# HGRN2 score levels: two chunks per product with one chunk's keys reversed, and keys and prefixes of later groups on ScalarE

## What is computed

```python
def hgrn2_chunk(S, inp):
    q, k, v, logf = inp
    G = jnp.cumsum(logf, axis=2)
    diff = G[:, :, :, None, :] - G[:, :, None, :, :]
    decay = jnp.exp(jnp.where(causal[None, None, :, :, None], diff, -jnp.inf))
    A = jnp.einsum('bhtd,bhtsd,bhsd->bhts', q, decay, k)
    o = jnp.einsum('bhts,bhsv->bhtv', A, v) + jnp.einsum('bhtd,bhdv->bhtv', q * jnp.exp(G), S)
    G_last = G[:, :, -1]
    S_new = jnp.exp(G_last)[..., None] * S + jnp.einsum(
        'bhsd,bhsv->bhdv', k * jnp.exp(G_last[:, :, None, :] - G), v)
    return S_new, o
```

## Time and profile before

| | us |
|---|---|
| runs: median (lowest to highest) | 708.96 (708.69 to 710.48) |
| profiled execution | 710.52 |
| its span, first to last instruction | 708.8 |
| busy in the span: TensorE products | 691.4 |
| TensorE weight loads | 661.7 |
| VectorE | 425.1 |
| GpSimd | 353.6 |
| ScalarE | 304.5 |
| mean granted TensorE clock | 0.995 of full speed |

### The profile page before, as it was taken

One profiled execution on the slowest core, in us unless ns is written; L12 is line 12 of the kernel. 1 busy time (PEld: TensorE's weight loads), 2 busy tenths in 40 slices (PEclk: granted clock), 3 DMA queues, 4 the chain that ended last, 5 costly groups with the idle time before them and its releaser, 6 DMA issues.

```text
span 708.8 us, 13435 instructions
## 1 busy us (share of the span) xinstructions
PE 691.4 (98%) x4822; PEld 661.7 (93%) x4822; DVE 425.1 (60%) x998; ACT 304.5 (43%) x860; POOL 353.6 (50%) x461
## 2 busy tenths in 40 slices
PE   7999999999999999999999999999999989999995
PEld 6799999999999999999999999999999988888884
DVE  5835346279882362698923645989336158776257
ACT  6644541635543516345444254455452343232333
POOL 5753233357572343476724333768243368765423
...
## 3 DMA queue, kind: packets, MB, share of 16 engines
...
## 4 chain that ended last, share of the span: by engine, by line
PE 84%; DVE 5%; POOL 3%; issue 2%; DMA 2%; SPq 1%; ACT 1%; POOLq 0%; DVEq 0%; ACTq 0%
PE proj L277 45%; PE proj L296 10%; PE mix L1720 5%; PE mix L1751 3%; PE mix L2197 3%; PE mix L2169 2%; PE mix L2209 2%; PE mix L2171 2%; PE mix L1701 2%; PE mix L896 1%; PE mix L1695 1%; PE mix L887 1%; PE mix L902 1%; PE mix L822 1%; PE mix L1691 1%
## 5 line engine op out<-in xcount | busy, mean ns | idle before, releaser
L277 PE MATMUL proj<-uTh,w_high 128*128 128x352 f32 (+4 forms) x768 | 261.7, 341 | 0.0
L277 PE MATMUL proj<-uTh,w_low 128*128 128x352 f32 (+4 forms) x768 | 245.7, 320 | 0.0
L277 PE MATMUL proj<-uTl,w_high 128*128 128x352 f32 (+4 forms) x768 | 245.3, 319 | 0.0
L277 PEld LDWEIGHTS proj<-uTh,w_high 128*128 128x128 f32 x768 | 145.1, 189 | 0.2
L277 PEld LDWEIGHTS proj<-uTl,w_high 128*128 128x128 f32 x768 | 145.1, 189 | 0.0
L277 PEld LDWEIGHTS proj<-uTh,w_low 128*128 128x128 f32 x768 | 144.3, 188 | 0.0
L322 POOL TENSOR_TENSOR w_low<-w_raw,w_high 128x256 fp32r<-128x256 f32 (+1 forms) x54 | 73.1, 1355 | 52.5 <-DVE decay L370 26.8
L1292 POOL TENSOR_TENSOR f_suffix<-f_suffix,f_prefix 128x192 f32<-128x192 f32 x84 | 54.3, 647 | 26.5 <-DVE f_prefix L1512 19.5
L1720 PEld LDWEIGHTS mix<-level_x 128*127 128x127 f32 (+6 forms) x448 | 54.3, 175 | 5.3 <-issue 2.9
L1720 PE MATMUL mix<-level_x 128*127 128x64 f32 (+6 forms) x448 | 54.1, 253 | 0.8 <-DVE level_x L1503 0.8
L1560 DVE SCALAR_TENSOR_TENSOR conv_out<-conv_in,hg_taps,conv_out 128x352 f32<-128x352 f32 (+2 forms) x81 | 52.5, 648 | 0.5
...
## 6 DMA issues: line engine op xcount, KB each, us to landing
...
```

The lines of the kernel that those rows point to most:

```text
L277: last = pe.matmul(acc[:, 0:tw], w[j % 2][:, k, :], u[:, k, t0:t0 + tw], start=(k == 0 and i == 0), stop=(k == KT - 1 and i == 2))
```

## The change

It does five things.

1. **Level products.** `X` becomes two pairs of tiles. `XK` (256 columns) holds chunk 0's keys in its first 128 columns; in its second 128 columns the even-block keys of chunk 1 stand in their places and those of chunk 2 in reversed order, which puts them on the places of the odd blocks. `XQ` (192 columns) holds the odd queries densely. One product of `XK`'s second half with the 128 queries of chunks 1 and 2 gives both chunks' scores; chunk 0 has a product of its own from group 1 on. The keys are no longer cut. GpSimd writes the even keys in two instructions, the second in reverse.
2. **Reversed tokens of chunk 2.** So that the scores of each group's last chunk have reversed keys throughout, `back` (128 columns) holds that chunk's reversed keys for m = 0 and then its reversed values for the transpose; `kf` is written in two instructions, its last 128 columns in reverse.
3. **Masks.** `mask_st` becomes `mask_diag`, `mask_odd` (with a reversed one for the last chunk, made by `flipped_masks` on GpSimd between two weight splits of the front phase) and `mask_lv` for the GDN phases; VectorE makes 15 copies in place of one cast.
4. **ScalarE makes keys and prefixes of groups 1 and 2** (`affine`), and the reversed blocks (`keys_back`, and a copy of the reversed values once the gram step 0 is done). VectorE's `start` remains for group 0.
5. **The squares** write to `on` instead of to a tile of their own.

```diff
-        pool.tensor_copy(mask_st[:, 0, :], ident[:, :]).then_inc(consts, 1)
+        for c in range(GC - 1):
+            pool.tensor_copy(mask_diag[:, c, :], ident[:, :]).then_inc(consts, 1)
...
+        def flipped_masks():
+
+            pool.memset(flipped[:, 0:LEVELS, :], 1.0).then_inc(flip_step, 1)
+            pool.memset(flip_diag, 0.0).then_inc(flip_step, 1)
...
+            for i in range(LEVELS):
+                b = 1 << i
+                pool.affine_select(out=cells(i), in_=cells(i), compare_op=ALU.is_ge, fill=0.0, base=b - P,
+                                   pattern=[[2 * b, P // (2 * b)], [0, b]], channel_multiplier=1).then_inc(flip_step, 1)
...
         early_low(3)
+        flipped_masks()
         early_low(4)
...
-        dve.tensor_copy(mask_st[:, 1:LEVELS + 1, :], mwork[:, 0:LEVELS, :])
+        for i in range(LEVELS):
...
+            for c in range(GC - 1):
+                dve.tensor_copy(mask_odd[:, i, c, :].rearrange("p (n b) -> p n b", b=b), odd)
+        dve.tensor_copy(mask_lv[:, :, :], mwork[:, BASE:LEVELS - 1, :])
...
-        X = [sb(f"level_x{i}", [P, GW], F32, st) for i in range(2)]
+        XK = [sb(f"level_k{i}", [P, 2 * P], F32, st) for i in range(2)]
+        XQ = [sb(f"level_q{i}", [P, GW // 2], F32, st) for i in range(2)]
+        back = sb("hg_back", [P, P], F32, st)
...
+            for t in XK:
+                pool.memset(t[:, 0:P], 0.0)
...
-                    xv_, kv_, sv_ = (halves(t[:, first(g):GW], b) for t in (X[n % 2], kk, suf))
-                    if i == 0:
-                        pool.tensor_copy(xv_[:, :, 0, :], kv_[:, :, 0, :]).then_inc(x_even, 1)
-                    else:
+                    if i:
                         pool.wait_ge(suf_done, n)
-                        pool.tensor_tensor(xv_[:, :, 0, :], kv_[:, :, 0, :], sv_[:, :, 0, :], ALU.mult
-                                           ).then_inc(x_even, 1)
+                    flipped_k = XK[n % 2][:, P:2 * P][:, ::-1]
+                    for dst, cs in ((XK[n % 2][:, first(g):2 * P], slice(first(g), 2 * P)), (flipped_k, slice(2 * P, GW))):
+                        xv_, kv_, sv_ = (halves(t, b)[:, :, 0, :] for t in (dst, kk[:, cs], suf[:, cs]))
+                        if i == 0:
+                            last = pool.tensor_copy(xv_, kv_)
+                        else:
+                            last = pool.tensor_tensor(xv_, kv_, sv_, ALU.mult)
+                    last.then_inc(x_even, 1)
...
-                pool.tensor_tensor(kf[:, :], kk[:, :], suf[:, :], ALU.mult).then_inc(kf_done, 1)
+                pool.tensor_tensor(kf[:, 0:2 * P], kk[:, 0:2 * P], suf[:, 0:2 * P], ALU.mult)
+                pool.tensor_tensor(kf[:, 2 * P:GW][:, ::-1], kk[:, 2 * P:GW], suf[:, 2 * P:GW], ALU.mult).then_inc(kf_done, 1)
...
+            def affine(dst, src, a, b):
+                return act.activation(dst, src, ACT.Identity, scale=fc[:, a:a + 1], bias=fc[:, b:b + 1])
+
+            def keys_back(g):
+                affine(back[:, :], hth[:, (g + 1) * GW - P:(g + 1) * GW][:, ::-1], 2, 1).then_inc(k_back, 1)
+
+            act.wait_ge(par, 3)
+            keys_back(0)
...
+                    if m == 0:
+                        full(act, plan, ("gram", g, 0))
+                        act.copy(back[:, :], hv[:, (g + 1) * GW - P:(g + 1) * GW][:, ::-1]).then_inc(v_back, 1)
...
+                if g + 1 < NG:
+                    act.wait_ge(qf_done, g + 1)
+                    act.wait_ge(tot_set, g + 1)
+                    affine(pre[:, :], hth[:, (g + 1) * GW:(g + 2) * GW], 1, 0).then_inc(pre_set, 1)
                 act.copy(vtok[:, :], full(act, plan, ("tv", g))[:, 0:GW]).then_inc(bank_free(plan, ("tv", g)), 1)
+                if g + 1 < NG:
+                    keys_back(g + 1)
+                    act.wait_ge(kf_done, g + 1)
+                    affine(kk[:, :], hth[:, (g + 1) * GW:(g + 2) * GW], 2, 1).then_inc(fk, 1)
                 act.copy(ktok[:, :], full(act, plan, ("tk", g))[:, 0:GW]).then_inc(bank_free(plan, ("tk", g)), 1)
...
-                if g + 1 < NG:
-                    start(g + 1)
...
-                        else:
-                            both = X[(LEVELS * g + m - 1) % 2][:, chunk(i)]
-                            keys = max(P - (1 << (m - 1)), HALF)
-                            last = pe.matmul(ap[0:keys, i * P // 2:(i + 1) * P // 2], both[:, 0:keys],
-                                             halves(both, 1 << (m - 1))[:, :, 1, :], start=True, stop=True)
+                    else:
+                        n = LEVELS * g + m - 1
+                        keys, odd = XK[n % 2], XQ[n % 2]
+                        if g:
+                            pe.matmul(ap[:, 0:P // 2], keys[:, 0:P], odd[:, 0:P // 2], start=True, stop=True)
+                        last = pe.matmul(ap[:, P // 2:GW // 2], keys[:, P:2 * P], odd[:, P // 2:GW // 2], start=True, stop=True)
```

82 lines of the change are left out of this document (51 added, 31 removed).

## The result

Twenty runs of each kernel: before 708.97 us (708.48 to 711.01), after **710.47 us** (709.65 to 711.58), ratio 1.0017 with a 95% interval of 1.0011 to 1.0023. That is slower by 1.2 us (0.8 to 1.6), inside the 0.3% that I called no change. I had forecast 704.1, with a range of 700.4 to 709.4: the sign and the range were both wrong. The profiled execution took 711.58 us, its span is 709.9 (before: 708.8).

A forecast was written before the change was run, and what follows sets the result against it. TensorE, busy 98% of the span, was taken as the bound. Terms -7.8 - 1.2 + 0.8 + 3.0 + 0.3 = -4.9 us, from a median of 708.96, gave 704.1 us, range 700.4 to 709.4.

The forecast's parts named there:

- The products: Joined level products on TensorE: -7.8 us over eight groups (1 and 2, four heads), -1.2 in the last head's group 0.
- In groups 1 and 2 [...] it is the bound: TensorE, busy 23.10 of 23.10 and 25.70 of 25.80 us in one head's groups 1 and 2, sets their pace.
- a shorter product only makes TensorE wait longer: I count 0: Group 0 of the first three heads, set by VectorE and GpSimd: no gain from joining (bound 1.2 us each).
- The second instruction on GpSimd: Even keys of a level written in two instructions: 0.25 us at TensorE per head in group 0, three heads, +0.8.
- I take 0.15, as the 64-element row is nearest: Extra GpSimd time per level for splitting the even keys: 0.15 us, bounds 0.05 and 0.6.
- Rival 3: Split on GpSimd costs much more than 0.15 us a level; zero effect at e = 0.42, 716 at 0.6; chance 0.12.
- in groups 1 and 2 it is hidden: GpSimd's second even-key instruction costs nothing there, as GpSimd is busy only 14.98 of 23.10 and 19.27 of 25.80 us.
- ScalarE: Added keys and prefixes (1.47 us) delay normalisation at group 1's end; TensorE waits 1.0 us in heads 0 to 2: +3.0.
- +0.3 in all: ScalarE's keys after group 0 nearly late for TensorE, and a reversed value block in group 1; bounds 0 and 0.9 us.
- Rival 2: VectorE and GpSimd also set the pace in groups 1 and 2, half the 7.8 lost: 708.0 us; chance 0.20.
- Front phase and masks: Extra mask instructions on GpSimd and copies on VectorE fit in idle time: 0 us (without cover, up to 2).

The follow-up runs named there:

- one_even: Changed kernel with one even-key instruction of 128 elements per level on GpSimd, chunk 2's level keys left out; 705.95 us, ratio 0.9945.
- dve_start_one_even: Changed kernel with keys and prefixes of groups 1 and 2 back on VectorE and one even-key instruction per level, chunk 2's left out; 703.20 us, ratio 0.9912.
- dve_start: Changed kernel with keys and prefixes of groups 1 and 2 back on VectorE, two even-key instructions kept; 710.27 us, ratio 1.0008.
- act_order: Changed kernel, same instructions, with ScalarE's queue at a group's end reordered (keys first, normalisation earlier); 710.45 us, ratio 1.0006.
- g0_plain_act_order: Changed kernel with ScalarE's queue at group ends reordered, group 0 unjoined and one clear of shared score cells; 708.02 us, ratio 0.9975.
- before_queue: Kernel before with two weight quarters moved out of GpSimd's levels of groups 0 and 1, third reciprocal root one level sooner; 711.01 us, ratio 1.0027.

## Why the prediction was wrong

**The products** (-7.8 and -1.2). The price of a product was right: 0.44 us a level, 0.96 in the last head's group 2 against 0.97 forecast, 0.93 over the levels of group 2 in head 0. What TensorE makes of it in heads 0 to 2 was not: with both added costs out they gain 0.73 in group 1 and 0.48 in group 2, so that what the -7.8 stood for is at most 3 x 1.21 + 0.96 + 0.95 = 5.5 us (with the last head's group 0 it makes the 6.2). The step that failed here is "In groups 1 and 2 [...] it is the bound": TensorE was busy 25.70 of 25.80 us in group 2, but VectorE was so close behind (22.74) that half of the gain there became a wait of 0.50 for gd_on. The 0.24 a head missing in group 1 stays open. The -1.2 of the last head's group 0 was not: -0.22, and -0.73 with both added costs out; what takes the other 0.5 there I did not find. In heads 0 to 2, "a shorter product only makes TensorE wait longer: I count 0" held (17.12 against 17.14).

**The second instruction on GpSimd** (+0.8), the step that failed first. "I take 0.15, as the 64-element row is nearest": after, the forms are

```profile
L1336 POOL TENSOR_TENSOR f_suffix<-f_suffix,f_prefix 128x192 f32<-128x192 f32 x84 | 52.1, 620 | 16.9 <-DVE f_prefix L1574 6.2 <-POOL level_k L1326 0.4
...
L1326 POOL TENSOR_TENSOR level_k<-hg_k,f_suffix 128x64 f32<-128x64 f32 x96 | 41.3, 440 | 0.9
...
L1326 POOL TENSOR_TENSOR level_k<-hg_k,f_suffix 128x128 f32<-128x128 f32 x48 | 26.3, 547 | 3.7 <-PE mix L1780 2.3
```

so the part of 64 elements costs 0.44, not 0.325: that was the row of another instruction, at another place. The right number was in the rows shown: the even-key instruction itself took 0.57 for 128 elements and 0.695 for 192, so 64 more elements cost 0.125 and the instruction as such 0.32, which makes 0.445 for one of 64. A split adds that 0.32 less 0.05, 0.27; measured 0.440 + 0.547 - 0.695 = 0.29, less 0.05 of overlap 0.24. Rival 3 had a dearer split, though not for its reason, since the reversal is free, and gave zero effect at e = 0.42. Yet the kernel was slower at under 0.3, because I measured the room where the chain ends, 1.2 us at the transposed factor, and not along it: GpSimd's suffix is what VectorE's prefix waits for, the prefix feeds the odd queries, and TensorE waits for those at gram steps 5 and 6, before the room at the end comes into play. GpSimd's idle time before the suffix fell from 26.5 to 16.9 us, while VectorE's wait for the suffix, ahead of its prefix, rose from 2.7 to 10.1 (rows below). And "in groups 1 and 2 it is hidden" failed in group 1: 0.62 a head, as much as the 0.60 in group 0, where I had counted 0.25. The term is +3.8 to +4.6, not +0.8.

**ScalarE** (+3.0). End of group 1 in ScalarE's order of time:

```profile
187.16 0.72 ACT L1474 ACTIVATE f_prefix<-hg_th,hg_fcur 128x384 f32<-128x384 f32 x1
187.76 0.49 ACT L1504 COPY hg_vtok<-mix 128x384 f32<-128x384 f32 x1
188.12 0.52 ACT L1474 ACTIVATE hg_back<-hg_th,hg_fcur 128x128 f32<-128x128 f32 x1
188.52 0.72 ACT L1474 ACTIVATE hg_k<-hg_th,hg_fcur 128x384 f32<-128x384 f32 x1
189.12 0.49 ACT L1509 COPY hg_ktok<-mix 128x384 f32<-128x384 f32 x1
189.48 0.66 ACT L1470 ACTIVATE hg_on<-mix,hg_rs 128x128 f32<-128x128 f32 x2
```

The three additions take 0.60 + 0.40 + 0.60 = 1.60 us from start to start, and I had 1.47. The Trainium skill (ScalarE: Activation LUTs, What ACT_TABLE_LOAD costs) had given an estimated 1.58 with its second pointer operand, and the trace agrees with it. The size at hg_on was right in the changed kernel: forecast 1.0 a head, 0.90 in the timelines (0.74 of it idle). By itself the move costs 2.1 us on the kernel before. What I had under "+0.3 in all" was larger: the keys of group 1 come 0.59 us late, since VectorE's totals, late through GpSimd, hold ScalarE's prefix up, and the keys stand behind it. The prefix in the change and in one_even, without the split:

```profile
163.93 0.71 ACT L1474 ACTIVATE f_prefix<-hg_th,hg_fcur 128x384 f32<-128x384 f32 x1 [0.98 <-DVE hg_tot L1670]
```

```profile
163.13 0.71 ACT L1473 ACTIVATE f_prefix<-hg_th,hg_fcur 128x384 f32<-128x384 f32 x1 [0.32 <-DVE hg_tot L1669]
```

**The wait that I did not have**: gd_on in group 2, 0.43 us in the change and 1.3 to 1.5 in dve_start, act_order and g0_plain_act_order, where something ahead of it was mended. The earlier trace rows gave GpSimd 19.27 and VectorE 22.74 of 25.80 us in that group and I took the rest for room. From one root to the next there was none to speak of: without the split VectorE is full and the stretch takes 12.80 us, with it GpSimd has no pause left and it takes 12.92. What the split adds to this wait comes ahead of the second root, which starts 0.23 us behind the group's first product in dve_start_one_even and 0.75 in dve_start; the rest, 0.50, is VectorE's pace.

**Rival 2** was right on VectorE's pace in group 2, for 0.5 us a head. On the contention that I had named beside it the rows say two things. The Trainium skill (GPSIMD Engine Reference, Key points) has GpSimd contend for shared SBUF interfaces with VectorE's instructions of two SBUF inputs. In the change VectorE's prefixes got longer, 530 to 615 ns, but its odd queries shorter: prefix and odd queries together were busy 91.8 us before

```profile
L1512 DVE TENSOR_TENSOR f_prefix<-f_prefix 128x192 f32<-128x192 f32 x84 | 44.5, 530 | 2.8 <-POOL f_suffix L1292 2.7
...
L1503 DVE TENSOR_TENSOR level_x<-hg_q,f_prefix 128x192 f32<-128x192 f32 x56 | 34.3, 613 | 1.5
...
L1503 DVE TENSOR_TENSOR level_x<-hg_q,f_prefix 128x128 f32<-128x128 f32 x28 | 13.0, 463 | 1.1
```

and are 90.0 after:

```profile
L1574 DVE TENSOR_TENSOR f_prefix<-f_prefix 128x192 f32<-128x192 f32 x84 | 51.7, 615 | 10.6 <-POOL f_suffix L1336 10.1
...
L1564 DVE TENSOR_TENSOR level_q<-hg_q,f_prefix 128x192 f32<-128x192 f32 x56 | 29.2, 522 | 1.5
...
L1564 DVE TENSOR_TENSOR level_q<-hg_q,f_prefix 128x128 f32<-128x128 f32 x28 | 9.1, 325 | 1.1
```

So with 28 us more work on GpSimd the two together did not get longer. As the odd queries are also written densely now, these rows don't tell the contention apart from that. Where GpSimd's work was moved next to a short instruction of VectorE, in before_queue, that instruction did get longer, 0.16 to 1.05 us. It has only one input; what stretches it no run isolates. Front phase and masks cost nothing, as forecast: the first group starts at 147.74 against 148.03.

In sum the forecast was -9.0 + 0.8 + 3.0 + 0.3. The runs show -6.2, +3.8 to +4.6 and +2.1, and the whole is +1.2, or 0.7 to 1.5 more than these add up to, about what the intervals of the ratios allow. The group lengths show one interplay that is real: the late keys of group 1 appear only with both costs in, and make group 0 of heads 0 to 2 0.67 us longer than the two costs do one by one.
